# Two-level down-projection: weight loads moved to another queue, a block of sums moved, one large read cut in sixteen

## The chip, the cores and the metric

One core of a Trainium2 chip (trn2). The metric is the device time of one execution in microseconds. The kernel before takes 2875.6 us (median of three runs, 2875.38 to 2876.66).

## The reference, cut to what matters

The program is two whole blocks in fp32: an attention block with an MLP, then a pooling/recurrence block with a mixture of experts. The change touches the MLP of the first block and nothing else:

```python
h = rms_norm(x, norm_mlp) * (1 + sc_f) + sh_f          # 1024 tokens x 1024
x = x + g_f * (square(relu(h @ w_mlp_in)) @ w_mlp_out)  # 1024 -> 4096 -> 1024
```

## The kernel before, in words

Everything about the change is in `stage_out_mlp`. The products are Strassen-like: a 2x2 block product is made of seven products m1 to m7 of sums of blocks, so the tensor engine (PE) does fewer products and the vector engine (DVE) more additions. After the attention's output projection come two stages.

**The up stage** (h @ w_mlp_in, relu, square). There are 32 pairs: 2 halves of the tokens times 16 pairs of hidden columns (`FPAIRS`). A pair n is seven products in the order m1, m5, m6, m7, m2, m4, m3 (`up_pair`, `product`, line 1343), four fp32 matmuls each (a matmul of fp32 is two records in the trace, so a product is 8 records). For each pair:

- SyncE (SP) loads the pair's 1 MB of weights into one of two buffers `w1s[n % 2]` (`pair_weights`, line 1201). The load of pair n+1 takes the buffer of pair n-1, so it waits until PE has done pair n-1.
- DVE makes four sums of the weights (`sums_of`, lines 1538 to 1543). m5, m6, m7 and m3 read them; m1, m2 and m4 read the raw weights.
- DVE takes the products out of the eight PSUM banks (`gather`, `add`, line 1568): u2 (product m6), u3 (m7), u4 and c22 (m5, the third and fourth taking), c11 (m2), c21 (m4), c12 (m3). A product can only start when the product eight places earlier has been taken.
- ScalarE (ACT) copies m1, then clamps and squares the four corners c22, c11, c21, c12 (lines 1503, 1513, 1516). In pairs 1 to 4 it also takes turned activations of the second token half first (`take_h`). In the second half of the tokens SP stores the squares to `hid_rows` (`hidden_store`, line 1218).

In the DVE program of before, the sums of pair n+1 stand ahead of all takings of pair n (line 1786).

Beside this runs **the preparation of the down weights**, in 16 sub blocks s. SP loads a sub block of 1 MB (`sub_load`, lines 1208 and 1209: 768 and 256 KB), DVE makes 45 more blocks of it in four steps (`sub_sums`, lines 1580 to 1595), SP stores 3.1 MB to `t_rows` in DRAM (`sub_store`, line 1213), and the next `sub_load` waits until that store has landed, since there is one buffer. DVE has the steps at fixed places of its program: `between(i)` of pair n is place 7n+i, and sub block s has its four steps at `made_from(s) = 18 + 49*s//4` and the three places after it, that is one sub block every 12.25 products or 1.75 pairs. i runs 0 (ahead of u2), 1 (ahead of u3), 2, 3, 4 (ahead of c11), 5, 6 (ahead of c12), and the first steps of four sub blocks in a row fall on i = 4, 2, 0, 5. `sub_store` stands at place +5 of the SP program and the next `sub_load` at place +8; `hidden_store(n-1)` stands at place i = 3 of pair n. SP runs its program strictly in order, and all of its transfers are in one queue. After the last store SP reads the residual back (line 1260, 4 MB).

**The down stage** (@ w_mlp_out) runs 14 passes: 2 halves of the tokens times the 7 outer products `OUTER`, each pass of 8 quads of 7 products of one matmul (line 1385). SP loads 896 KB of `t_rows` for each quad into a ring of four buffers (`down_sums_in`, line 1231), each as soon as the quad four earlier is done. The first and the last two quads of a pass are interleaved product by product, so those are done nearly together. The activations of the second half come back from `hid_rows` by `hidden_load` (line 1236), two DMAs of 4 MB, issued in the SP program behind the loads of quads 43 and 51 (passes 5 and 6); pass 7 is the first that reads them. In the last pass PE also turns the first half of the residual, 8 blocks of 4 transposes (`turn_residual`, line 1399), into bank 7; ACT copies each out (line 1521) before the next.

Of the kernel before, what the change touches and what calls it, by code (L numbers as in the profile page):

```python
# [1031 lines left out]
def stage_out_mlp(nc, main, tail, early, w1, w2, w_head, t_rows, hid_rows, x_rows, xres, ada_acc, b_ada, cols, modc, gates, ones, ident):  # L1032
# [9 lines left out]
    with Scope(nc, "mlp") as s:  # L1042
# [136 lines left out]
        def operand_there(eng, g):  # L1179
            h, name = g // HALF_PASSES, OUTER[g % HALF_PASSES]  # L1180
            if name in ("m5", "m6", "m7", "m3"):
                eng.wait_ge(side_made, side_at(h, name))
            elif h:
                eng.wait_ge(hid_in[0 if name == "m1" else 1], 16)
            else:
                eng.wait_ge(squared, 4 * FPAIRS)

        ended_at = [0]
        for g in range(PASSES):
# [2 lines left out]
        with nc.Block() as block:  # L1192
            @block.sync
            def _(sp):
                def pair_weights(n):
                    if n == 1:
                        sp.wait_ge(out_part, len(out_parts))
                    if n >= 2:
                        sp.wait_ge(up, 7 * (n - 1))
                        sp.wait_ge(summed, 4 * (n - 1))  # L1200
                    sp.dma_start(w1s[:, n % 2, :, :], w1[n % FPAIRS]).then_inc(w1_in[n % 2], 16)

                def sub_load(s):
                    if s:
                        sp.wait_ge(sub_out, 16 * s)
                    else:
                        sp.wait_ge(parked, 16 * TT)
                    sp.dma_start(sub_all[:, 0:3, 0:4, :], w2[s // 2, s % 2, :, 0:3]).then_inc(sub_in, 16)
                    sp.dma_start(sub_12, w2[s // 2, s % 2, :, 3]).then_inc(sub_in, 16)

                def sub_store(s):
                    sp.wait_ge(sub_made, 8 * s + 8)
                    sp.dma_start(t_rows[:, s // 2, :, s % 2, :].rearrange("o p n -> p o n"),
                                 sub_all[:, :, 1:8, :].rearrange("p o i n -> p o (i n)")).then_inc(sub_out, 16)

                def hidden_store(n):
                    sp.wait_ge(squared, 4 * n + 4)
                    sp.dma_start(hid_rows[n - FPAIRS], staged[:, n % 2, :]).then_inc(hid_out[n % 2], 16)

                def down_sums_in(n):  # L1220
                    g, j = n // QUADS, n % QUADS
                    if n < RING:
                        sp.wait_ge(sub_out, 16 * SUBS)
                        sp.wait_ge(up, 7 * (2 * FPAIRS - 1 if n < 2 else 2 * FPAIRS))
                        sp.wait_ge(summed, 4 * (2 * FPAIRS - 1 if n < 2 else 2 * FPAIRS))
                    if n == 3:
                        for out in hid_out:
                            sp.wait_ge(out, 8 * FPAIRS)
                    if n >= RING:
                        quad_done(sp, (n - RING) // QUADS, (n - RING) % QUADS)  # L1230
                    sp.dma_start(ring[n % RING][:, 0:14 * P], t_rows[IN_PLACE[OUTER[g % HALF_PASSES]], j].rearrange("p c n -> p (c n)")
                                 ).then_inc(t_in[n % RING], 16)

                def hidden_load(o):
                    sp.wait_ge(side_made, side_at(0, "m7" if o == 0 else "m3"))
                    sp.dma_start(main[:, :, 2 * o * NB:(2 * o + 2) * NB],
                                 hid_rows.rearrange("(j o) p c -> o p j c", o=2)[o]).then_inc(hid_in[o], 16)

                for g, off in enumerate((2 * D, 5 * D)):
                    sp.dma_start(brow[:, g, :], b_ada[off:off + D].partition_broadcast(P)).then_inc(brow_in, 16)  # L1240
                pair_weights(0)
                pair_weights(1)
                sp.wait_ge(xn_done, TT)
                for t in range(TT):
                    sp.dma_start(x_rows[t * P:(t + 1) * P, :], xres[:, t, :]).then_inc(parked, 16)
                for n in range(2 * FPAIRS):
                    if 1 <= n < 2 * FPAIRS - 1:
                        pair_weights(n + 1)
                    for i in range(7):
                        at = 7 * n + i  # L1250
                        if at in sub_stores:
                            sub_store(sub_stores[at])
                        if at in sub_loads:
                            sub_load(sub_loads[at])
                        if i == 3 and n > FPAIRS:
                            hidden_store(n - 1)
                        if at == made_from(SUBS - 1) + 6:
                            sp.wait_ge(sub_out, 16 * SUBS)
                            for t in range(TT):
                                sp.dma_start(xres[:, t, :], x_rows[t * P:(t + 1) * P, :]).then_inc(x_back, 16)  # L1260
                    if n == 2 * FPAIRS - 1:
                        down_sums_in(0)
                        down_sums_in(1)
                hidden_store(2 * FPAIRS - 1)
                down_sums_in(2)
                down_sums_in(3)
                for n in range(RING, PASSES * QUADS):
                    down_sums_in(n)
                    if n == 5 * QUADS + RING - 1:
                        hidden_load(0)  # L1270
                    if n == 6 * QUADS + RING - 1:
                        hidden_load(1)
                    if n == 13 * QUADS + RING - 1:
                        sp.wait_ge(side_made, side_at(1, "m3"))
                        flat = w_head.rearrange("p n k c -> p (n k c)")
                        sp.dma_start(main[:, 2:6, HEAD_AT:2 * D], flat[:, 0:28 * P].rearrange("p (r c) -> p r c", r=4)).then_inc(head_in, 16)
                        sp.dma_start(main[:, 6, HEAD_AT:HEAD_AT + 4 * P], flat[:, 28 * P:32 * P]).then_inc(head_in, 16)
                sp.wait_ge(head_in, 32)

            @block.tensor  # L1280
            def _(pe):
# [120 lines left out]
                def down_pass(g):  # L1402
                    operand_there(pe, g)
                    last_pair = 2 * FPAIRS - 1
                    for i, name in enumerate(PRODUCTS):
                        if g:
                            pe.wait_ge(copied, 7 * (g - 1) + i + 1)
                        elif i == 0:
                            pe.wait_ge(part, part_at(last_pair - 1, "c12"))
                        elif i == 1:  # L1410
                            pe.wait_ge(taken, last_pair + 1)
                        else:
                            pe.wait_ge(part, part_at(last_pair, LAST_READ[PRODUCTS[i - 1]]))
                        for j in range(2):
                            down_product(g, j, name)
                    for j in range(2, QUADS - 2):
                        for name in PRODUCTS:
                            down_product(g, j, name)
                        if g == PASSES - 1:
                            turn_residual(2 * j - 4)  # L1420
                            turn_residual(2 * j - 3)
                    for name in PRODUCTS:
                        for j in range(QUADS - 2, QUADS):
                            down_product(g, j, name)
# [23 lines left out]
            def _(act):  # L1448
# [48 lines left out]
                for half in range(2):  # L1497
                    for j in range(FPAIRS):
                        n = half * FPAIRS + j
                        act.wait_ge(up, up_at(n, "m1"))  # L1500
                        if n:
                            act.wait_ge(part, part_at(n - 1, "c11"))
# [27 lines left out]
            def _(dve):  # L1530
# [66 lines left out]
                def gather(n, j, next_tokens):  # L1597
# [20 lines left out]
                    dve.wait_ge(part, part_at(n, "u3"))  # L1618
                    corner_free("c22")
                    add(n, "c22", corner["c22"], "m5", u3)  # L1620
                    between(4)
                    corner_free("c11")
                    add(n, "c11", corner["c11"], "m2", first_copy)
# [26 lines left out]
                def side_sums(g):  # L1650
                    h, name = g // HALF_PASSES, OUTER[g % HALF_PASSES]
                    X, Y = by_side
                    if name == "m5":
                        if h:
                            dve.wait_ge(hid_in[0], 16)
                            dve.wait_ge(hid_in[1], 16)
                            dve.wait_ge(whole, 7 * (g - HALF_PASSES + 3))
                        else:
                            dve.wait_ge(up, 14 * FPAIRS)
# [122 lines left out]
                for half in range(2):  # L1782
                    for j in range(FPAIRS):
                        n = half * FPAIRS + j
                        if n + 1 < 2 * FPAIRS:
                            every(sums_of(n + 1))
                        else:
                            inner_sums(0, 0)
                        gather(n, j, next_tokens if n == FPAIRS - 1 else iter(()))
                for g in range(PASSES):  # L1790
# [2011 lines left out]
```

## Time and profile before

| | before |
|---|---|
| median of three runs | 2875.6 us |
| the profiled execution | 2869.83 us, of which the span 2868.1 us |
| granted TensorE clock, whole span | 0.964 |
| PE busy | 2613.7 us, 91% |
| DVE busy | 1636.3 us, 57% |
| ACT busy | 871.7 us, 30% |
| DMA over the span | 476.06 MB, mean 166 GB/s |

The trace has the start of each instruction from the start of the span, its duration, and what an engine waited for before it. The granted clock is a share of 2.4 GHz. SPq is the issue of a DMA on SyncE; it is not the transfer. "8 records" of line 1343 are one product.

### The profile page before, as it was taken

To read this page: it belongs to the slowest core of one execution; us is meant where nothing else is said; L and a number is where in the kernel's file an instruction comes from. 1 tells how busy PE (TensorE), PEld (TensorE's weight loads), DVE (VectorE), ACT (ScalarE), POOL (GpSimd) and SP (SyncE) were. 2 spreads that over 40 slices of the span, in tenths; PEclk is the share of its full clock that TensorE was granted. 3 is DMA by queue.
4 is the path that set the end of the run, shared out by engine and by line. 5 is a ranking of instruction groups with operands and counts; after the bars stand their busy time and mean duration, and the time that the engine had idled before them with its cause. 6 is when DMAs were issued, how large, how long until landed. Compare 5 with 4: busy or idle time off the path is not lost. (4 is left out here: it accounts for less than half of the span.)

```text
span 2868.1 us, 55655 instructions
## 1 busy us (share of the span) xinstructions
PE 2613.7 (91%) x22330; PEld 1890.7 (66%) x22330; DVE 1636.3 (57%) x4094; ACT 871.7 (30%) x2171; POOL 305.5 (11%) x411
## 2 busy tenths in 40 slices
PE   6999999999887887779889998999999989999996
PEld 4888766654676666668778846777777755544443
DVE  5443277775544644544635536888888857522225
ACT  3111166642221221211011124666666610200002
POOL 0000023310000000000000000111111100353312
PEclk9999999999999988889999999999999989999998
DMA  5010143320355456578888731000000020599995
GB/s 237 31 59 30 59 159 122 126 97 1 124 209 229 185 221 239 210 265 308 327 305 300 304 151 61 28 28 28 3 28 28 18 107 30 206 394 402 401 383 198
DMA packets 138035, 476.06 MB, mean 166 GB/s; under 512 B 10928, under 2 KB 20656, under 8 KB 128832
## 3 DMA queue, kind: packets, MB, share of 16 engines
q1 hardware_dynamic: 129536, 447.99, 41.8%
q0 software_dynamic: 8256, 24.65, 2.3%
q8 instruction: 174, 2.85, 0.4%
q14 instruction: 69, 0.57, 0.1%
HBM read 375.55 MB, written 97.06 MB: 165 GB/s over the span
## 5 line engine op out<-in xcount | busy, mean ns | idle before, releaser
L2204 PE MATMUL mixing_ps<-all_main,pre_ws 64*64 64x256 f32 x3072 | 247.1, 379 | 0.0
L3291 PE MATMUL ex_ps<-all_main,ex_xT 128*128 128x512 f32 x496 | 223.4, 593 | 2.4 <-DVE ex_xT L3449 2.1
L1343 PE MATMUL mlp_ps<-all_main,all_early 128*128 128x256 f32 x512 | 141.4, 425 | 90.0 <-DMA all_early<-in_w 73.7
L1343 PEld LDWEIGHTS mlp_ps<-all_main,all_early 128*128 128x128 f32 x512 | 107.4, 213 | 112.7 <-DMA all_early<-in_w 79.3
L1513 ACT ACTIVATE all_gates<-all_gates 128x256 f32<-128x256 f32 x128 | 52.2, 408 | 381.0 <-DVE all_gates L1568 380.9
L1538 DVE TENSOR_TENSOR mlp_w2s<-all_early 128x512 f32<-128x512 f32 x32 | 22.0, 688 | 250.4 <-DMA all_early<-in_w 250.4
L3291 PEld LDWEIGHTS ex_ps<-all_main,ex_xT 128*128 128x128 f32 x496 | 91.7, 190 | 107.1 <-issue 100.7
L1343 PE MATMUL mlp_ps<-all_tail,mlp_w2s 128*128 128x256 f32 x512 | 131.2, 411 | 27.4 <-DVE all_gates L1568 27.4
L2204 PEld LDWEIGHTS mixing_ps<-all_main,pre_ws 64*64 64x64 f32 x3072 | 133.3, 134 | 19.3 <-issue 0.3
L1343 PEld LDWEIGHTS mlp_ps<-all_tail,mlp_w2s 128*128 128x128 f32 x512 | 106.9, 211 | 48.3 <-issue 29.1
L254 PE MATMUL qkv_ps<-qkv_wq,h_hT 128*128 128x256 f32 x576 | 134.3, 386 | 2.9 <-DVE h_hT L547 2.9
L1385 PE MATMUL mlp_ps<-mlp_w2s 128*128 128x256 f32 x448 | 126.2, 385 | 0.0
L254 PEld LDWEIGHTS qkv_ps<-qkv_wq,h_hT 128*128 128x128 f32 x576 | 111.5, 194 | 19.6 <-issue 4.1
L1343 PE MATMUL mlp_ps<-all_main,mlp_w2s 128*128 128x256 f32 x512 | 122.3, 382 | 0.0
L1385 PE MATMUL mlp_ps<-mlp_w2s,all_main 128*128 128x256 f32 x336 | 97.3, 385 | 19.3 <-DMA mlp_w2s<-t_rows 19.1
L3241 POOL DMA_INDIRECT all_main<-h_rows,ex_idx x112 | 106.6, 951 | 49.5 <-issue 27.0
L1890 POOL MEMSET pool_blank<- 128x1024 f32 x1 | 1.0, 954 | 1032.3 <-POOLq L60 1032.3
L1643 DVE TENSOR_TENSOR mlp_w2s<-all_main 128x512 f32<-128x512 f32 x28 | 19.4, 691 | 156.2 <-PE mlp_ps L1385 155.8
L1343 PEld LDWEIGHTS mlp_ps<-all_main,mlp_w2s 128*128 128x128 f32 x512 | 98.8, 193 | 13.9
L2626 DVE STREAM_TRANSPOSE all_tail<-all_tail 64x128 f32<-64x128 f32 (+1 forms) x336 | 100.5, 304 | 9.3
L2899 PE MATMUL mixing_ps<-all_main 128*128 128x512 f32 x224 | 102.2, 600 | 0.7 <-PEq L2136 0.7
L2468 ACT COPY all_tail<-mixing_ps 128x256 f32<-128x256 f32 (+2 forms) x264 | 86.2, 347 | 37.3 <-PE mixing_ps L2306 33.6
(512 smaller groups left out, 5680.0 us busy)
## 6 DMA issues: line engine op xcount, KB each, us to landing
all_main<-in_w_gu SPq DMA_DIRECT2D x31, 2048.0 KB, 14.9
t_rows<-all_xres SPq DMA_DIRECT2D x16, 3136.0 KB, 10.1
mlp_w2s<-t_rows SPq DMA_DIRECT2D x56, 896.0 KB, 6.1
all_early<-in_w SPq DMA_DIRECT2D x32, 1024.0 KB, 8.1
all_early<-t_rows SPq DMA_DIRECT2D x28, 896.0 KB, 6.2
all_tail<-t_rows SPq DMA_DIRECT2D x28, 896.0 KB, 5.5
att_wa<-in_w_ada SPq DMA_DIRECT2D x32, 512.0 KB, 3.9
all_early<-in_w_d SPq DMA_DIRECT2D x16, 1024.0 KB, 17.2
```

The lines of the kernel that those rows point to most:

```text
L254: last = nc.tensor.matmul(ps[:, bank_of[c, i, name], 0:HN], lhsT=weights(k), rhs=moving(k), start=k == 0, stop=k == HK - 1)
L1343: last = nc.tensor.matmul(ps[:, bank(n, name), 0:QB], lhsT=weights(k), rhs=moving(k), start=k == 0, stop=k == HK - 1)
L1385: last = nc.tensor.matmul(ps[:, PRODUCTS.index(name), 0:QB].rearrange("p (c t) -> p c t", c=2), lhsT=lhsT, rhs=rhs, start=j == 0, stop=j = ...
L1513: nc.scalar.activation(corner[name], corner[name], ACT.Relu).then_inc(clamped, 1)
L1538: yield nc.vector.tensor_tensor(S[0], A21, A22, ALU.add).then_inc(summed, 1)
L1643: nc.vector.tensor_tensor(s1, x21, x22, ALU.add).then_inc(in_made, 1)
L2204: last = nc.tensor.matmul(ps[heads(m), banks[half], 0:UT], lhsT=ws[heads(half), n, k, heads(m)], rhs=columns(k, heads(half)), start=(k == ...
L2468: nc.scalar.copy(dst, src).then_inc(steps.sem, 1)
L2626: ins_of(*args, **kw).then_inc(dve_w.sem, 1)
L2899: last = nc.tensor.matmul(ps[:, 2 * (t % 2) + n, :], lhsT=mixT[:, k, t * P:(t + 1) * P], rhs=ws[:, k, n * NB:(n + 1) * NB], start=(k == 0) ...
L3241: nc.gpsimd.indirect_dma_start(out=xg[:, n, a * QD:(a + 1) * QD], out_offset=None, in_=h_quarters, in_offset=bass.IndirectOffsetOnAxis(ap= ...
L3291: last = nc.tensor.matmul(pg[:, n % 2, :], lhsT=(xT[:, n % 2, :] if x is None else x)[:, k * P:(k + 1) * P], rhs=gu[n][:, k, :], start=(k ...
```

## The change

Four edits, all in `stage_out_mlp`. The up weights of pair n+1 are loaded from ScalarE's queue, at the start of its work for pair n, that is behind the squares of pair n-1; the first two loads stay on SP. DVE makes the sums of pair n+1 behind the fourth taking (c22) of pair n, no longer ahead of the first. The second half's activations are read in 16 DMAs of 512 KB, one behind the load of each of the quads 46 to 61. In the last pass the two turnings of a quad stand behind m5 and behind m2, no longer both behind m3.

```diff
--- before.py
+++ after.py
@@ -1181,9 +1181,17 @@
             if name in ("m5", "m6", "m7", "m3"):
                 eng.wait_ge(side_made, side_at(h, name))
             elif h:
-                eng.wait_ge(hid_in[0 if name == "m1" else 1], 16)
+                eng.wait_ge(hid_in[0 if name == "m1" else 1], 16 * QUADS)
             else:
                 eng.wait_ge(squared, 4 * FPAIRS)
+
+        def pair_weights(eng, n):
+            if n == 1:
+                eng.wait_ge(out_part, len(out_parts))
+            if n >= 2:
+                eng.wait_ge(up, 7 * (n - 1))
+                eng.wait_ge(summed, 4 * (n - 1))
+            eng.dma_start(w1s[:, n % 2, :, :], w1[n % FPAIRS]).then_inc(w1_in[n % 2], 16)
 
         ended_at = [0]
         for g in range(PASSES):
@@ -1192,14 +1200,6 @@
         with nc.Block() as block:
             @block.sync
             def _(sp):
-                def pair_weights(n):
-                    if n == 1:
-                        sp.wait_ge(out_part, len(out_parts))
-                    if n >= 2:
-                        sp.wait_ge(up, 7 * (n - 1))
-                        sp.wait_ge(summed, 4 * (n - 1))
-                    sp.dma_start(w1s[:, n % 2, :, :], w1[n % FPAIRS]).then_inc(w1_in[n % 2], 16)
-
                 def sub_load(s):
                     if s:
                         sp.wait_ge(sub_out, 16 * s)
@@ -1231,21 +1231,18 @@
                     sp.dma_start(ring[n % RING][:, 0:14 * P], t_rows[IN_PLACE[OUTER[g % HALF_PASSES]], j].rearrange("p c n -> p (c n)")
                                  ).then_inc(t_in[n % RING], 16)
 
-                def hidden_load(o):
+                def hidden_load(o, j):
                     sp.wait_ge(side_made, side_at(0, "m7" if o == 0 else "m3"))
-                    sp.dma_start(main[:, :, 2 * o * NB:(2 * o + 2) * NB],
-                                 hid_rows.rearrange("(j o) p c -> o p j c", o=2)[o]).then_inc(hid_in[o], 16)
+                    sp.dma_start(main[:, j, 2 * o * NB:(2 * o + 2) * NB], hid_rows[2 * j + o]).then_inc(hid_in[o], 16)
 
                 for g, off in enumerate((2 * D, 5 * D)):
                     sp.dma_start(brow[:, g, :], b_ada[off:off + D].partition_broadcast(P)).then_inc(brow_in, 16)
-                pair_weights(0)
-                pair_weights(1)
+                pair_weights(sp, 0)
+                pair_weights(sp, 1)
                 sp.wait_ge(xn_done, TT)
                 for t in range(TT):
                     sp.dma_start(x_rows[t * P:(t + 1) * P, :], xres[:, t, :]).then_inc(parked, 16)
                 for n in range(2 * FPAIRS):
-                    if 1 <= n < 2 * FPAIRS - 1:
-                        pair_weights(n + 1)
                     for i in range(7):
                         at = 7 * n + i
                         if at in sub_stores:
@@ -1266,10 +1263,10 @@
                 down_sums_in(3)
                 for n in range(RING, PASSES * QUADS):
                     down_sums_in(n)
-                    if n == 5 * QUADS + RING - 1:
-                        hidden_load(0)
-                    if n == 6 * QUADS + RING - 1:
-                        hidden_load(1)
+                    if 5 * QUADS + 6 <= n < 6 * QUADS + 6:
+                        hidden_load(0, n - 5 * QUADS - 6)
+                    if 6 * QUADS + 6 <= n < 7 * QUADS + 6:
+                        hidden_load(1, n - 6 * QUADS - 6)
                     if n == 13 * QUADS + RING - 1:
                         sp.wait_ge(side_made, side_at(1, "m3"))
                         flat = w_head.rearrange("p n k c -> p (n k c)")
@@ -1416,9 +1413,8 @@
                     for j in range(2, QUADS - 2):
                         for name in PRODUCTS:
                             down_product(g, j, name)
-                        if g == PASSES - 1:
-                            turn_residual(2 * j - 4)
-                            turn_residual(2 * j - 3)
+                            if g == PASSES - 1 and name in ("m5", "m2"):
+                                turn_residual(2 * j - 4 + ("m5", "m2").index(name))
                     for name in PRODUCTS:
                         for j in range(QUADS - 2, QUADS):
                             down_product(g, j, name)
@@ -1497,6 +1493,8 @@
                 for half in range(2):
                     for j in range(FPAIRS):
                         n = half * FPAIRS + j
+                        if 1 <= n < 2 * FPAIRS - 1:
+                            pair_weights(act, n + 1)
                         act.wait_ge(up, up_at(n, "m1"))
                         if n:
                             act.wait_ge(part, part_at(n - 1, "c11"))
@@ -1618,6 +1616,8 @@
                     dve.wait_ge(part, part_at(n, "u3"))
                     corner_free("c22")
                     add(n, "c22", corner["c22"], "m5", u3)
+                    if n + 1 < 2 * FPAIRS:
+                        every(sums_of(n + 1))
                     between(4)
                     corner_free("c11")
                     add(n, "c11", corner["c11"], "m2", first_copy)
@@ -1652,8 +1652,8 @@
                     X, Y = by_side
                     if name == "m5":
                         if h:
-                            dve.wait_ge(hid_in[0], 16)
-                            dve.wait_ge(hid_in[1], 16)
+                            dve.wait_ge(hid_in[0], 16 * QUADS)
+                            dve.wait_ge(hid_in[1], 16 * QUADS)
                             dve.wait_ge(whole, 7 * (g - HALF_PASSES + 3))
                         else:
                             dve.wait_ge(up, 14 * FPAIRS)
@@ -1782,9 +1782,7 @@
                 for half in range(2):
                     for j in range(FPAIRS):
                         n = half * FPAIRS + j
-                        if n + 1 < 2 * FPAIRS:
-                            every(sums_of(n + 1))
-                        else:
+                        if n + 1 == 2 * FPAIRS:
                             inner_sums(0, 0)
                         gather(n, j, next_tokens if n == FPAIRS - 1 else iter(()))
                 for g in range(PASSES):
```

## Rows read from the trace of the kernel before

**Rows 1.** Windows, the up stage: us, busy per engine (instructions), clock, DMA share, GB/s

```profile
737.00:1284.00 547.00, 429.59 (x1825) 365.47 (x1824) 275.42 (x495) 119.96 (x307) 0.00 (x0) 0.90 0.58 218
```

**Rows 2.** Waits, up stage, PE: us in total, times, longest

```profile
PE mlp_ps L1343 <- DMA all_early<-in_w: 73.7, 14, 16.1
PE mlp_ps L1343 <- DVE all_gates L1568: 43.7, 12, 8.8
```

**Rows 3.** Waits of SP's own queue, up stage

```profile
SPq L1213 <- DVE all_xres L1595: 266.4, 16, 21.0
SPq L1208 <- DMA t_rows<-all_xres: 142.0, 15, 10.7
```

**Rows 4.** Timeline around one PE stall: start us, us, engine, line, operation, records [idle before]

```profile
1120.60 0.38 SPq L1213 DMA_DIRECT2D t_rows<-all_xres  x1
...
1130.03 0.38 SPq L1208 DMA_DIRECT2D all_xres<-in_w  x1
...
1131.07 0.35 SPq L1201 DMA_DIRECT2D all_early<-in_w  x1
...
1139.37 0.69 DVE L1538 TENSOR_TENSOR mlp_w2s<-all_early 128x512 f32<-128x512 f32 x1 [16.81 <-DMA all_early<-in_w]
1139.39 1.22 PE L1343 MATMUL mlp_ps<-all_main,all_early 128*128 128x256 f32 x2 [8.29 <-DMA all_early<-in_w]
```

**Rows 5.** Timeline: two products, one clamping, steps of two sub blocks

```profile
1085.35 0.68 DVE L1580 TENSOR_TENSOR all_xres<-all_xres 128x512 f32<-128x512 f32 x1
...
1092.00 1.09 DVE L1595 TENSOR_TENSOR all_xres<-all_xres 128x896 f32<-128x896 f32 x1
...
1110.24 0.68 DVE L1580 TENSOR_TENSOR all_xres<-all_xres 128x512 f32<-128x512 f32 x1
...
1113.67 1.89 PE L1343 MATMUL mlp_ps<-all_main,all_early 128*128 128x256 f32 x8
...
1115.39 1.89 PE L1343 MATMUL mlp_ps<-all_tail,all_early 128*128 128x256 f32 x8
...
1121.66 0.42 ACT L1513 ACTIVATE all_gates<-all_gates 128x256 f32<-128x256 f32 x1 [6.98 <-DVE all_gates L1568]
```

**Rows 6.** Timeline, first and last of the 16 stores of sub blocks

```profile
796.30 0.38 SPq L1213 DMA_DIRECT2D t_rows<-all_xres  x1
...
1242.43 0.38 SPq L1213 DMA_DIRECT2D t_rows<-all_xres  x1
```

**Rows 7.** DMA issues: count, KB each, median us to landing; last, line 1201 alone

```profile
t_rows<-all_xres SPq DMA_DIRECT2D x16, 3136.0 KB, 10.1
...
all_xres<-in_w SPq DMA_DIRECT2D x16, 768.0 KB, 4.6
...
DMA to landing us min/median/max: 4.8/8.1/13.7
```

**Rows 8.** Timeline, a stall ahead of the first sub block, one behind the last

```profile
771.10 3.75 PE L1343 MATMUL mlp_ps<-all_main,all_early 128*128 128x256 f32 x8 [8.80 <-DVE all_gates L1568]
...
1269.05 0.69 DVE L1538 TENSOR_TENSOR mlp_w2s<-all_early 128x512 f32<-128x512 f32 x1 [24.66 <-DMA all_early<-in_w]
```

**Rows 9.** Timeline, down stage: ring loads that mark the ends of passes

```profile
1358.55 1.49 SPq L1231 DMA_DIRECT2D mlp_w2s<-t_rows  x1
...
1382.72 5.93 SPq L1231 DMA_DIRECT2D mlp_w2s<-t_rows  x2
...
1408.73 0.36 SPq L1231 DMA_DIRECT2D mlp_w2s<-t_rows  x1
...
1476.68 0.36 SPq L1231 DMA_DIRECT2D mlp_w2s<-t_rows  x1
```

**Rows 10.** Windows, down stage: without and with a read of 4 MB

```profile
1364.00:1384.00 20.00, 20.00 (x94) 17.64 (x93) 10.37 (x12) 2.60 (x7) 0.00 (x0) 1.00 0.80 299
...
1444.00:1464.00 20.00, 12.12 (x54) 10.31 (x53) 11.20 (x18) 0.00 (x0) 0.00 (x0) 0.88 1.01 409
```

**Rows 11.** Timeline, last pass: one of four second turnings

```profile
1634.80 0.65 PE L1399 MATMUL mlp_ps<-all_ident,all_xres 128*128 128x128 f32 x4 [0.68 <-ACT all_main L1521]
```

## The prediction

> **What bounds the kernel now.** I read the windows by stage first. The up stage takes 547 us at a granted clock of 0.90 [rows 1]. Then the pace of an undisturbed product: two neighbours start 1.72 us apart [rows 5], so seven are 12.1 us and the 224 products of 32 pairs 387 us; with 7 us for the turnings in it (eight at 0.9 us), PE needs 394 us. The stage thus loses 153 us. PE's waits name 117 of them: 73.7 for the weights themselves, 43.7 for DVE's takings [rows 2], and the rest is mostly the slow level behind a stall (8 records in 3.75 us at 1.2 GHz [rows 8], 1.89 at 2.4 GHz [rows 5]). The takings are late for the same reason: DVE stands ahead of all takings of a pair and waits for the next pair's weights. Then SP's own waits: 266.4 us for the last step of a sub block and 142.0 us for the landing of its store [rows 3]. One stall shows how these meet: the store leaves at 1120.60, SP stands at the next `sub_load` until 1130.03, and only then, at 1131.07, sends the weights whose buffer had been free since PE passed to the next pair, some 12 us before; DVE gets them at 1139.37 after 16.81 us, PE has stood for 8.29 us [rows 4]. So the bound of the stage is the order of SP's program. In the down stage an undisturbed pass is 24.17 us (1358.55 to 1382.72), and the two passes with the 4 MB reads take 67.95 us together (1408.73 to 1476.68), 19.6 more than two plain ones [rows 9].
>
> **Loads on ScalarE's queue: what comes next.** At the start of its pair n ACT has squared c12 of pair n-1, so PE and the sums are long past what the two added waits ask; they cost nothing, and behind them stand only the copy of m1 and the squares. The issue costs on SP 0.35 us [rows 4]; no row shows one on ACT. 30 of them lie in an engine busy for 120 of 547 us [rows 1], price 0 (bounds: below nothing is excluded, an issue cannot shorten ACT's work; above, 30 x 1.1 us, SP's longest issue, in the idle time anyway). Two loops are then left, and the longer one sets the stage.
>
> *Weight loop.* Load lands, four sums at about 0.61 us spacing, each 0.69 [rows 4]: 2.5 us; then c11, c21, c12, and ACT's three pairs of clamp and square at 0.8 us (twice 0.4 [rows 5]) behind c11: 2.9 us; then the next load. Steps of a sub block on places 4 to 6 come between: a sub block's steps are 7.1 us of DVE (4 x 0.68 + 4 x 1.08 [rows 5]), 4.0 us a pair, 3/7 of them there, of which ACT's lag hides a quarter: 1.3 us. The load: 4.8 us at best, 8.1 median, 13.7 worst, with SP's stores ahead of it in one queue [rows 7]. In a queue of its own it no longer stands behind 3.1 MB. 1 MB at the 409 GB/s that a full window moves [rows 10] is 2.6 us; alone 4.8, at half the rate 7.4; I take 7.0. Loop: 7.0 + 2.5 + 2.9 + 1.3 = 13.7 us a pair. PE wants 12.1.
>
> *Sub block loop.* Steps, store, load, one after the other in one buffer. The steps with the takings between them take 7.8 us from the first step to the store (1085.35 to 1093.1) or 10.4 (1110.24 to the store at 1120.60) [rows 4, 5]; half each, 9.1. The change keeps that: the sums leave one place and come into another (i = 2 now has them inside). The store takes 10.1 us to land [rows 7]; a weight load runs beside it now, 2.6 us of the same 16 DMA engines, in about three stores of four: 12.1. The next load takes 0.4 + 4.9, with the same sharing in four of ten cases 6.2. Sum 27.4 us for 1.75 pairs, 15.7 us a pair. It is the longer loop, and it is the next bound; DVE will stand at the first step of a sub block (L1580) for its load, which it never does now. Now a sub block takes (1242.43 - 796.30)/15 = 29.74 us [rows 6]. Fifteen intervals: 15 x (29.74 - 27.4) = **-35.1 us**.
>
> The Trainium skill, *DMA: Bandwidth & Descriptors*, "Queues, rings and completion order", says each DMA engine alternates between the queues that have work, packet by packet. That fits the half rate taken; no run here has shown two busy queues of this kind.
>
> **Sums behind the fourth taking.** Costs no DVE time. It frees u2, u3, u4 and c22 from the wait for weights, so PE's banks of m6, m7 and m5 come free on time; what then waits behind the weights is c11, c21 and c12, whose banks are needed only eight products (13.8 us) later, and through them the next load: that is in the weight loop above. With the loads in time it also delays S for m5 of the next pair: weights landing at 9 us of a 12.1 us pair give the first sum at 9.7, needed at 13.8. Price inside the loops 0; if the weights land late, m5 stands 1 to 5 us, once in two pairs, in the time that the sub block loop leaves PE idle anyway.
>
> **Both ends of the stage.** Ahead of the first sub block PE stands 8.8 us and pays 1.9 us at the slow level [rows 8], since the load of pair 2 is sent behind eight stores of x_rows. From ACT it is sent about 5 us earlier and lands beside them: that stall goes. By the durations above: the load of pair 2 is sent at 752.8 and lands at 760.5; that of pair 3 goes behind pair 1's squares, which ACT makes behind the two turned blocks, at 766.8, and lands at 773.8; sums to 776.3, the steps and takings 8.4 us, first store at 784.7 for 796.30: **-11.6**. Behind the last store, now at 1242.43, the stage takes 41.5 us more to 1283.9; in them the last weights stand behind the 4 MB residual, and DVE waits 24.66 us [rows 8]. With those weights sent by ACT, PE has 2.3 pairs left: 2.3 x 12.1 = 28 and a microsecond: 29. **-12.5**. Up stage: -59 us, 488 for 547.
>
> **Sixteen pieces.** Each quad of 3.02 us loads 0.9 MB, at a DMA share of 0.80: 2.4 us; a window full of the reads moves 409 GB/s at share 1.01 [rows 10], so 8.4 MB take 20.5 us, 1.28 us a piece. Over 16 quads the DMAs need 16 x (2.4 + 1.28) = 58.9 us and PE 48.3. 10.6 stay, less one to two us that the ring holds in store: 9. The two large reads now cost 19.6 [rows 9]. 19.6 - 9 = **-10.6** (bounds 0, the same bytes cost the same, and -19.6, all hidden). The pieces are all sent by quad 1 of pass 7, so pass 8 does not wait for them.
>
> **Turnings apart.** PE stands 0.68 us at the second turning of a quad, four times [rows 11]; with three products (1.3 us) between, ACT's copy is done: **-2.7**.
>
> **Sum.** -59.2 - 10.6 - 2.7 = -72.5; I give 2 us back for m1 and m5 run at the slow level where they are now on a path: -70.5. From the profiled execution (span 2868.1, 1.7 around it, 2869.8) that is 2799.3; the median of before is 5.8 us higher, and I state the forecast against it: 2875.6 - 70.5 = **2805**.
>
> **Rivals.**
> 1. *The sub block loop is shorter than I price it*, the two queues share without loss: 9.1 + 10.1 + 5.3 = 24.5. Then the weight loop (13.7 x 1.75 = 24.0) is as long, and 15 x (29.74 - 24.7) = 75.6 in place of 35.1: 2805 - 40.5 = 2764. For it: the DMA share of the stage is only 0.58 [rows 1]. Against: the loads must fall somewhere, and the store fills 12 of each 27 us. Chance 0.19.
> 2. *Moving the issue gives nothing, the transfers being what is late.* The weights land as late as now since the store and they need the same engines; only the down stage gains: 2875.6 - 13.3 = 2862. Against: of the 16.81 us in rows 4, 10 are SP's wait, in which the load was not sent. Chance 0.12. The Trainium skill, same page, "Issuing engines are not separate DMA queues", says issuing from several engines only saves the sequencer's time; by that rule this is the result. The 142.0 us of rows 3 are just time of the sequencer, so row and rule can both hold.
> 3. *Slower: the weight loop closes on itself.* Before, a load waited for PE alone; now it waits for squares that wait for c12, that waits for the sums, that wait for the load before. If the store holds the load back as it does in one queue (4.26 MB at 409 GB/s and the 2.2 us of a load alone that are not bytes: 12.6; worst seen 13.7 [rows 7]), the loop is 12.6 + 6.7 = 19.3 us a pair, 618 us in place of 547: +71, less 13.3 in the down stage: 2933. It decides from a landing of 10.4 us on, where the loop is today's 17.1 a pair; with the gains of the down stage from 10.8. For it: nothing here shows how two queues share. Chance 0.07.
> 4. *Same:* the landing at that point, 0.02.
>
> **How the numbers follow.** Forecast 0.60, own range 2784 to 2830 (a loop of 26 to 29, pieces -5 to -17). The range takes in half of rival 1 and stops short of rivals 2 and 3: 2760 to 2852. About 0.2% is what a measurement here can tell. Faster 0.91, same 0.02, slower 0.07.
>
> **What the profile after would show.** SP's wait for a landed store stays, but no weights stand behind it; L1201 issues on ACT. The longest wait of DVE is for the sub block's load at L1580 and for weights at L1538 of some 3 to 5 us a time, not 14 to 25. Stores of sub blocks 27 us apart; the stage near 488 us; PE's clock still under 1. Passes 5 and 6 near 58 us together; no idle at the second turning. If the stores come 25 us apart, rival 1; if L1201 takes over 10 us to land with the stage over 547, rival 3; if L1538 waits as before, rival 2.

## The result

The changed kernel takes 2796.2 us (median of four, 2793.1 to 2797.7) for 2875.6: ratio 0.9722, 95% interval 0.9705 to 0.9739, 79 us less. The forecast was 2805 (range 2760 to 2852). The time came out as foreseen; two of the reasons given for it did not hold, and the experiments below took them apart.

Of the page of the changed kernel, the time by engine and two of its DMA issues:

```profile
span 2791.3 us, 55669 instructions
...
PE 2605.0 (93%) x22330; PEld 1878.7 (67%) x22330; DVE 1637.7 (59%) x4094; ACT 876.9 (31%) x2171; POOL 305.9 (11%) x411
...
t_rows<-all_xres SPq DMA_DIRECT2D x16, 3136.0 KB, 11.3
...
all_early<-in_w ACTq DMA_DIRECT2D x30, 1024.0 KB, 7.2
```

The work is the same and the span is 76.8 us shorter. The up stage in windows (same columns as [rows 1]), and PE's and DVE's waits in it, answering [rows 2]:

```profile
736.50:1209.20 472.70, 416.92 (x1825) 355.61 (x1823) 279.02 (x497) 125.87 (x309) 0.00 (x0) 0.94 0.68 252
```

```profile
PE mlp_ps L1340 <- DMA all_early<-in_w: 37.5, 16, 5.8
PE mlp_ps L1340 <- issue: 14.2, 6, 6.1
PE mlp_ps L1340 <- DVE all_gates L1566: 2.5, 1, 2.5
```

```profile
DVE mlp_w2s L1536 <- DMA all_early<-in_w: 84.0, 19, 7.5
DVE all_xres L1578 <- DMA all_xres<-in_w: 44.3, 12, 9.0
```

The stage is 472.7 us for 547, at a granted clock of 0.94 for 0.90. PE's waits for takings fell from 43.7 to 2.5 us, those for weights from 73.7 to 37.5 (14.2 more are at m5, for the first of the sums, and stand under "issue"). DVE now waits at L1578 for a sub block's load, which it never did. The first and the last store of a sub block, answering [rows 6]:

```profile
782.46 0.38 SPq L1213 DMA_DIRECT2D t_rows<-all_xres  x1
...
1178.43 0.38 SPq L1213 DMA_DIRECT2D t_rows<-all_xres  x1
```

They are (1178.43 - 782.46)/15 = 26.40 us apart for 29.74, and PE begins the down stage 30.8 us behind the last for 41.7. SP still waits for the landing of the stores, as in [rows 3], and longer:

```profile
SPq L1213 <- DVE all_xres L1593: 215.9, 16, 16.7
SPq L1208 <- DMA t_rows<-all_xres: 163.3, 15, 13.4
```

One turn of the weight loop, from the timeline (ACTq is the issue of a DMA on ScalarE):

```profile
841.91 0.33 ACTq L1194 DMA_DIRECT2D all_early<-in_w  x1
...
850.51 0.69 DVE L1536 TENSOR_TENSOR mlp_w2s<-all_early 128x512 f32<-128x512 f32 x1 [6.21 <-DMA all_early<-in_w]
850.53 1.99 PE L1340 MATMUL mlp_ps<-all_main,all_early 128*128 128x256 f32 x8 [2.24 <-DMA all_early<-in_w]
...
853.05 0.42 DVE L1566 TENSOR_TENSOR all_gates<-mlp_ps,mlp_spare 128x256 f32<-128x256 f32 x1
...
856.25 0.42 DVE L1566 TENSOR_TENSOR all_gates<-mlp_ps,mlp_small 128x256 f32<-128x256 f32 x1
...
857.14 0.42 ACT L1514 ACTIVATE all_main<-all_gates 128x256 f32<-128x256 f32 x1
857.21 0.33 ACTq L1194 DMA_DIRECT2D all_early<-in_w  x1
```

Load out at 841.91, landed at 850.5, four sums, c11 at 853.05, c12 at 856.25 with steps of a sub block between, its square, and the next load at 857.21: 15.3 us round, with PE standing 2.24.

### The profile page after: what moved, and what is told of

Its sections match the earlier page's. It is cut to its first block and busy times, and to the rows that moved or that the text cites. A ratio compares the mean times of both kernels' runs of the same rounds, so it can differ in the third digit from the quotient of the medians.

```text
span 2791.3 us, 55669 instructions
## 1 busy us (share of the span) xinstructions
PE 2605.0 (93%) x22330; PEld 1878.7 (67%) x22330; DVE 1637.7 (59%) x4094; ACT 876.9 (31%) x2171; POOL 305.9 (11%) x411
## 5 line engine op out<-in xcount | busy, mean ns | idle before, releaser
L1340 PE MATMUL mlp_ps<-all_main,all_early 128*128 128x256 f32 x512 | 132.8, 405 | 40.1 <-DMA all_early<-in_w 37.5
L1340 PEld LDWEIGHTS mlp_ps<-all_main,all_early 128*128 128x128 f32 x512 | 101.2, 201 | 61.9 <-DMA all_early<-in_w 44.2
L1340 PE MATMUL mlp_ps<-all_tail,mlp_w2s 128*128 128x256 f32 x512 | 126.5, 404 | 14.3 <-issue 14.2
L1382 PE MATMUL mlp_ps<-mlp_w2s,all_main 128*128 128x256 f32 x336 | 97.4, 384 | 12.4 <-DMA mlp_w2s<-t_rows 10.9
L1382 PEld LDWEIGHTS mlp_ps<-mlp_w2s 128*128 128x128 f32 x448 | 86.1, 193 | 12.0
## 6 DMA issues: line engine op xcount, KB each, us to landing
t_rows<-all_xres SPq DMA_DIRECT2D x16, 3136.0 KB, 11.3
```

The source lines that it names most:

```text
L1340: last = nc.tensor.matmul(ps[:, bank(n, name), 0:QB], lhsT=weights(k), rhs=moving(k), start=k == 0, stop=k == HK - 1)
L1382: last = nc.tensor.matmul(ps[:, PRODUCTS.index(name), 0:QB].rearrange("p (c t) -> p c t", c=2), lhsT=lhsT, rhs=rhs, start=j == 0, stop=j = ...
```

## Experiments

All were timed in three rounds against the kernel before. "Up stage" is from the first product of pair 0 to the first product of the down stage.

### Which of the two edits of the up stage did it

`e3_down_only`: only the edits of the down stage. Its diff against the changed kernel takes back both of these:

```diff
-                        if 1 <= n < 2 * FPAIRS - 1:
-                            pair_weights(act, n + 1)
...
+                    if 1 <= n < 2 * FPAIRS - 1:
+                        pair_weights(sp, n + 1)
...
-                    if n + 1 < 2 * FPAIRS:
-                        every(sums_of(n + 1))
...
+                        if n + 1 < 2 * FPAIRS:
+                            every(sums_of(n + 1))
```

> The kernel before with only the edits of the down stage: 16 pieces and turnings apart. Theory: passes 5 to 7 take 85.2 us as in the changed kernel for 93.0, the turnings give 2.7: 10.5 us less, 2865, and the 5 us by which other passes of the changed kernel were longer belong to that execution or to the up stage. Rival: the pieces or the earlier end cost those 5 us in the other passes too: 2870.

Measured: 2864.4 us, ratio 0.9968 (0.9950 to 0.9985), 9 us less. The theory (2865) was right. Its down stage takes 361.9 us for 371.8 before, and its up stage 549 for 547.

`e1_sums_back`: of the two, only the sums are put back; the loads stay on ScalarE's queue.

> The changed kernel with one part undone: the sums of pair n+1 stand again ahead of all takings of pair n; the loads stay on ScalarE's queue. Theory (the weight loop closes over DVE and ACT): land 7.0, sums 2.5, seven takings 2.7, steps of sub blocks 4.0, last squares 1.5 us make 17.7 us a pair, no better than the 17.1 of before: the up stage takes 530 to 566 us for 472.7 in the changed kernel, 2855 to 2885 us in all. Rival (the queue alone does the work): up stage within 10 us of the changed kernel's, 2796 to 2806 us.

Measured: 2898.0 us, ratio 1.0076 (1.0053 to 1.0100). **The change of queue alone makes the kernel slower**, by 34 us against `e3_down_only`; the up stage takes 577 us, more than the 530 to 566 that I had put it at. Its loads land in 8.5 us in the median, so the queue is not slow; they leave late. One turn in its timeline:

```profile
1011.14 0.69 DVE L1536 TENSOR_TENSOR mlp_w2s<-all_early 128x512 f32<-128x512 f32 x1 [5.49 <-DMA all_early<-in_w]
...
1016.96 3.41 PE L1340 MATMUL mlp_ps<-all_tail,mlp_w2s 128*128 128x256 f32 x8 [3.80 <-DVE all_tail L1549]
...
1022.66 0.42 ACT L1511 ACTIVATE all_gates<-all_gates 128x256 f32<-128x256 f32 x1 [15.66 <-DVE all_gates L1566]
...
1025.44 0.33 ACTq L1194 DMA_DIRECT2D all_early<-in_w  x1
...
1033.61 0.69 DVE L1536 TENSOR_TENSOR mlp_w2s<-all_early 128x512 f32<-128x512 f32 x1 [8.85 <-DMA all_early<-in_w]
```

From landed weights to the next load 14.3 us (this pair also has token sums in it): all takings of the pair and all four squares lie between. The load's 8 us come on top, 22.5 us in this turn; over the whole stage a pair takes 18.0 us (577 / 32) for the 17.7 of the theory.

`e2_loads_back`: of the two, only the loads are put back on SP.

> The changed kernel with the other part undone: loads of up weights on SyncE again at their old place, sums behind the fourth taking. Theory: PE's 43.7 us of waits for takings go, the 73.7 us of waits for weights stay, as SP still stands at the store of a sub block: up stage about 505 to 515 us, 2830 to 2842 in all. Rival (the place of the sums does the work, queue irrelevant): up stage under 480 us, 2796 to 2806 in all.

Measured: 2792.0 us, ratio 0.9709 (0.9679 to 0.9739), the same as the changed kernel. The rival was right: **the place of the sums alone brings the whole gain**, 72 us beyond `e3_down_only`. SP's order had not changed here, and yet PE's waits for weights fell. First PE's waits in `e3_down_only`, then PE's and DVE's in this run:

```profile
PE mlp_ps L1342 <- DMA all_early<-in_w: 73.2, 14, 16.9
PE mlp_ps L1342 <- DVE all_gates L1566: 39.1, 11, 8.7
```

```profile
PE mlp_ps L1342 <- DMA all_early<-in_w: 43.4, 11, 13.6
PE mlp_ps L1342 <- issue: 14.4, 5, 4.1
...
DVE mlp_w2s L1536 <- DMA all_early<-in_w: 66.4, 9, 17.6
```

The windows of both up stages (columns as in [rows 1]), `e3_down_only` first:

```profile
736.50:1285.50 549.00, 436.77 (x1825) 370.15 (x1825) 275.21 (x494) 120.01 (x307) 0.00 (x0) 0.88 0.57 217
```

```profile
740.00:1215.00 475.00, 416.99 (x1824) 358.50 (x1824) 276.82 (x494) 121.77 (x307) 0.00 (x0) 0.94 0.67 251
```

The stage is 74 us shorter: 39 us of waits for takings are gone, 30 of those for weights, 14 came at m5 (for the sums), and PE is busy for 20 us less with the same products, at a granted clock of 0.94 for 0.88.

The stores of its sub blocks are 25.5 us apart (790.95 to 1173.96), nearer than in the changed kernel. Counted from the first product of the stage, the changed kernel wins 5 us ahead of the first store and 10 behind the last, and gives 13 back in between, so its up stage is 3 us shorter; its down stage is 6 us longer (366.3 for 360.0).

### Was SyncE's order a bound at all

`e5_pool_loads` sends the loads of pairs 2 to 31 from GpSimd, which has nothing else to do in this stage, and `e8_pool_sums_back` does so with the sums at the old place:

```diff
+            @block.gpsimd
+            def _(pool):
+                for n in range(1, 2 * FPAIRS - 1):
+                    pair_weights(pool, n + 1)
```

> As the run with loads on GpSimd's queue, but the sums of the next pair ahead of all takings again, as in the kernel before. It tells apart what bound the kernel before. Theory A (SyncE's order, on which the prediction rested): with the loads out of SP's order and out of the squares' way most of the gain is there without moving the sums: up stage 485 to 500 us for 547, 2805 to 2825 in all. Theory B (DVE's order: it stands for the next weights with all takings behind it): up stage 530 us or more, 2845 to 2870.

Measured: 2805.0 us, ratio 0.9757 (0.9738 to 0.9776), up stage 486 us. Theory A gave this, at the lower end of its range. So a load that waits for neither SP's stores nor ScalarE's squares brings 59 us beyond `e3_down_only` with the sums unmoved; its loads land in 5.3 us in the median for 8.3, and DVE waits 56.5 us for them for 254.7 in `e3_down_only`. How much of the 59 us is the earlier issue and how much the shorter landing, no run separates. The loss of the kernel before had two links, SP late with the load and DVE standing for it with all takings behind it, and cutting either one takes most of it away. The cut must not close a new loop: with the loads on ScalarE's queue and the sums unmoved (`e1_sums_back`) it did.

> The changed kernel with the loads of up weights of pairs 2 to 31 on GpSimd's queue, which waits for nothing but PE and the sums, not for ScalarE's squares. Theory (in the changed kernel the loop over the squares holds the loads back): loads leave 2 to 6 us sooner, PE's 37.5 us of waits for weights in the up stage mostly go, 25 to 35 us less: 2761 to 2771. Rival (the sub block loop is the bound): stores of sub blocks stay 26.4 us apart, 2790 to 2800.

Measured: 2795.2 us, ratio 0.9724 (0.9708 to 0.9740), no gain over the changed kernel. The rival was right, and the waits say how: PE's for weights are gone, and the sub block's load takes their place.

```profile
PE mlp_ps L1345 <- issue: 57.6, 10, 10.9
...
PE mlp_ps L1345 <- DMA all_early<-in_w: 0.3, 1, 0.3
```

```profile
DVE all_xres L1586 <- DMA all_xres<-in_w: 107.7, 16, 13.3
```

The stores stay 26.6 us apart (782.51 to 1182.05). DVE stands at the sub block with the sums behind it, and PE stands at m5 for the sums; the longest wait in the timeline shows it, though the profile files it under "issue":

```profile
1012.29 0.69 DVE L1586 TENSOR_TENSOR all_xres<-all_xres 128x512 f32<-128x512 f32 x1 [13.30 <-DMA all_xres<-in_w]
...
1015.50 0.68 DVE L1544 TENSOR_TENSOR mlp_w2s<-all_early 128x512 f32<-128x512 f32 x1
...
1016.28 2.05 PE L1345 MATMUL mlp_ps<-all_tail,mlp_w2s 128*128 128x256 f32 x4 [10.92 <-issue]
```

The weight loop had been freed; the sub block loop held.

### Cutting the sub block loop, three times in vain

`e4_split_store` cuts each store of a sub block in two; the next load waits for the first part alone:

```diff
+                    for lo, hi, done in ((0, 3, sub_first), (3, 7, sub_out)):
+                        sp.dma_start(t_rows[lo:hi, s // 2, :, s % 2, :].rearrange("o p n -> p o n"),
+                                     sub_all[:, lo:hi, 1:8, :].rearrange("p o i n -> p o (i n)")).then_inc(done, 16)
```

> The changed kernel with each store of a sub block cut into two DMAs (3 and 4 of 7 outer blocks); the next sub block's load waits for the first alone. Theory (the sub block loop is the bound now): its store term falls from about 11 to 6.5 us, stores come 24 us apart for 26.4, then the weight loop of 13.7 us a pair sets them: 15 x 2.4 = 36 us less, 2760; DVE's waits for the sub block's load (44.3 us) go nearly to nothing. Rival (the weight loop is already the bound): no change, 2790 to 2800.

Measured: 2792.5 us, ratio 0.9716 (0.9685 to 0.9748): no gain. Its DMA issues:

```profile
t_rows<-all_xres SPq DMA_DIRECT2D x16, 1344.0 KB, 4.9
...
all_xres<-in_w SPq DMA_DIRECT2D x16, 256.0 KB, 10.9
```

SP waits only 66.0 us for landed stores, but the load then lands in 10.9 us for 5.8 in the changed kernel: it stands behind the second part in SP's queue. 4.9 + 10.9 = 15.8 us from the store's issue to the landed load, for 11.3 + 5.8 = 17.1 in the changed kernel. The stores stay 26.5 us apart, although the exchange is 1.3 us shorter: the weight loads now land in 8.3 us for 7.2, and PE waits 44.5 us for them for 37.5. The wait moved. So this run did not decide what it was made for.

`e6_sub_pool` and `e7_sub_pool_sp` send the sub block's load from GpSimd's queue, so that no bytes stand ahead of it in its own; the latter has the weights back on SP.

> The changed kernel with each sub block's store in two DMAs and the next sub block's load on GpSimd's queue behind the first of them, so that it stands behind no bytes of the second. From the store's issue to the landed load 16.7 us in the changed kernel (15.8 with the store cut alone); here about 5 + 6 = 11. Theory (sub block loop is the bound): stores 24 us apart for 26.4, 36 us less, 2760. Rival (it is not): 2790 to 2800.

> The same cut of the sub block loop, but the up weights' loads back on SyncE's queue, where now no wait for a landed store stands ahead of them. Theory: both loops are cut, stores 22.5 to 24 us apart, up stage about 440 to 450 us, 2755 to 2765. Rival (transfers share the engines, so something always lands late): 2785 to 2800.

Measured: 2798.0 us (ratio 0.9738, 0.9717 to 0.9759) and 2798.6 (0.9751, 0.9724 to 0.9778): no gain. The load in a queue of its own still lands late:

```profile
all_xres<-in_w POOLq DMA_DIRECT2D x16, 256.0 KB, 10.5
```

4.9 + 10.5 = 15.4 us; in `e7_sub_pool_sp` the load takes 11.1, together 16.0. The expected 11 us were wrong, and so were both theories: stores came 26.7 and 26.1 us apart. The first store part, the load and the second part still share the engines, with the weights besides. In neither run is it shown what each queue got; what is shown is that the buffer's exchange takes 15 to 17 us in any order of the same transfers, as long as all of it lies between two groups of steps.

### Opening both loops

`e9_early_act` changes what lies between. The blocks 1 to 3 of each group are ready after the second of the four steps and are stored then; the next load needs only them to have landed and DVE to be done, and the rest of the store goes behind that load. Only the third step of the next sub block waits for it.

```diff
+                        if at - 3 in sub_firsts:
+                            sub_store(sub_firsts[at - 3], 1, 4, 4, sub_first)
+                        if at in sub_stores:
+                            if sub_stores[at] + 1 < SUBS:
+                                sub_load(sub_stores[at] + 1)
+                            sub_store(sub_stores[at], 4, 8, 8, sub_out)
```

> The changed kernel with the sub block loop opened: the blocks that are ready after the second of four steps are stored at once, and the next sub block's load goes behind the fourth step, beside the store of the rest, for which only the next block's third step waits. Load weights as changed, from ScalarE. Theory (in the changed kernel the weight loop and the sub block loop are about equally long, so freeing one alone gave nothing): now the weight loop of 13.7 us a pair is left, up stage about 445 to 460 us for 472.7, 2765 to 2785. Rival (something common to all, bytes or DVE, is the floor): 2790 to 2800.

Measured: 2766.9 us, ratio 0.9617 (0.9590 to 0.9644), up stage 445 us, as the theory had it. PE waits 32.8 us, all for weights: the weight loop is what is left.

`e10_early_pool` has GpSimd's loads of weights besides:

> Both loops opened: sub blocks as in the run with the early store, and the up weights of pairs 2 to 31 from GpSimd's queue, which does not wait for squares. Theory (two loops, nothing else): sub block loop about 19 us for the 21.2 that PE needs, so PE sets most of it, up stage 410 to 435 us, 2735 to 2760. Rival (a floor common to all): 2785 to 2800.

Measured: **2716.6 us**, ratio 0.9436 (0.9409 to 0.9463), the fastest of all and better than the theory's 2735 to 2760. Its up stage in windows (columns as in [rows 1]), and PE's only wait in it:

```profile
736.50:1138.80 402.30, 396.54 (x1827) 347.07 (x1825) 278.64 (x497) 122.10 (x307) 16.10 (x30) 0.99 0.83 296
```

```profile
PE mlp_ps L1353 <- issue: 5.4, 2, 2.9
```

The window is 402 us, the stage itself 401 by its first products; PE is busy for 396.5 of it, at a clock of 0.99: PE is the bound of the stage now. Each loop freed alone gave 1 us (`e5_pool_loads`, no more than noise) and 29 us (`e9_early_act`); together 80.

`e11_early_sp` has the weights on SP:

> The early store with the up weights loaded from SyncE's queue as in the kernel before, sums behind the fourth taking. SyncE now waits for no long store, so its order costs little. Theory: as with GpSimd's queue within 10 us, 2740 to 2770. Rival (SyncE's order still holds the weights back): 2780 to 2800.

Measured: 2749.2 us, ratio 0.9557 (0.9527 to 0.9588), in the range of the theory, but 33 us from GpSimd's queue where it had said 10, so SP's order still costs something: PE waits 28.2 us for weights. It is 18 us better than ScalarE's queue.

`e12_open_sums_back` is `e10_early_pool` with the sums at the old place:

> The kernel with both loops opened (early store, loads on GpSimd's queue), but the sums of the next pair again ahead of all takings. What is the place of the sums worth when nothing else is late? Theory: the load leaves at the start of a pair and lands 7.7 us later, DVE stands for it until 8 us into the pair and then has takings, sums and steps to make up, so c22's bank comes free up to 3 us late in every second pair: 20 to 40 us more than with the sums behind the fourth taking, 2737 to 2757. Rival (the place only mattered since the loads were late): within 8 us of 2717.

Measured: 2763.9 us, ratio 0.9625 (0.9609 to 0.9641): 47 us more, above the theory's 20 to 40 and far from the rival. The place of the sums is worth something of its own, since PE then waits for banks:

```profile
PE mlp_ps L1353 <- DVE all_gates L1582: 27.8, 10, 5.7
```

## Why the prediction was right, and where it was not

- **What bounds the kernel.** I called the order of SP's program the bound. `e8_pool_sums_back` shows it was one of two links; `e2_loads_back` shows that most of the loss goes with SP's order untouched. Rows 2 to 4 show the chain in the order of one stall, and there SP's wait comes last; that SP itself was waiting for DVE (the 266.4 us of [rows 3]), which was waiting for weights, I read and did not follow round. A ring of waits has no first member, and can be cut at any link.
- **Sums behind the fourth taking: price 0.** This step failed. Alone it brings 72 us. I saw that it frees PE's banks (the 43.7 us of [rows 2]) and put that inside the loops. By bank waits alone it should have been some 44 us. The rest is 30 us less of waits for weights, of which 14 come back at m5, and 20 us that PE is busy less at the higher granted clock. That weights come sooner because the steps of the sub blocks, and with them SP's stores and loads, do so fits the stores (25.5 us apart for 29.9) but was not tested by itself.
- **Loads on ScalarE's queue: the source of the gain.** This step failed too. Alone it costs 34 us, and beside the moved sums it gives nothing that can be told (2796.2 and 2792.0). Rival 3 named the mechanism, loads gated by squares that wait for the load before, but I made it hang on a slow landing. Landings were fast (7.2 us median, 9.8 at most, where I took 7.0), and what decides it is how many takings lie between landed weights and the last square.
- **The two loops.** Right. I gave 27.4 us for the sub block loop; stores came 26.4 apart. Of its terms the store was 11.3 for 12.1. I gave 13.7 us a pair for the weight loop, 24.0 for 1.75 pairs; `e9_early_act`, where it is the only one left, takes 445 us for the stage, 13.9 a pair. By these lengths opening the weight loop alone should give nothing (`e5_pool_loads`: 1 us) and opening the sub block loop alone at most 15 x (26.4 - 24.0) = 36 us (`e9_early_act`: 29). What the sum lacked is that the two meet: when the exchange of the sub block got 1 to 2 us shorter in `e4_split_store` and `e6_sub_pool`, the weights landed 1 us later and the stores stayed as far apart.
- **Both ends of the stage.** Ahead of the first store -13.8 us for my -11.6, behind the last -10.9 for -12.5.
- **Up stage in sum.** -74.3 us (472.7 for 547.0) for my -59.2: nearly all of the difference is the one microsecond in each of 15 intervals.
- **Sixteen pieces.** -10.6 foreseen. In the changed kernel passes 5 to 7 take 85.2 us for 93.1, 7.9 less, but passes 0 to 3 take 5.7 more (104.1 for 98.4), so that its down stage is only 5.5 shorter (366.3 for 371.8). `e3_down_only` has 83.5 us in passes 5 to 7, 9.6 less. The term holds. The prediction had no term for the early passes: they take 98.4 to 100.4 us in the five kernels that load the up weights from SP and 99.7 to 104.2 in the nine that don't, one execution each, so the longer early passes seem to go with the moved queue and not with the pieces or the sums. By what way is open; the first two loads of the ring land 9.6 and 10.2 us after their issue in the changed kernel, 5.6 and 7.3 before.
- **Turnings apart.** -2.7: at the second turnings PE does not wait any more, seen in the timeline of the last pass, but the term was not measured by itself.
- **Rival 2** did not come true: 2796.2 us, not 2862. Its rule in the Trainium skill (*DMA: Bandwidth & Descriptors*, "Issuing engines are not separate DMA queues") says another issuing engine saves only the time that the sequencer takes to start the DMA. The runs do not agree: an issue takes 0.3 to 0.5 us here, and by the issuing engine alone `e8_pool_sums_back` gains 59 us and `e1_sums_back` loses 34. Those come with the waits that stand ahead of the issue in each engine's program and, in `e8_pool_sums_back`, with the shorter landing. Only beside the moved sums did the queue make no difference (`e2_loads_back`).

The number came out although the shares were wrong: I gave the gain of a ring of waits to the link that I had cut in thought first. A calculation that has both edits in it and prices the loops that remain does not need the shares. Some luck was in it too: the up stage gave 15 us more than foreseen and the down stage 8 less, and these errors partly cancel.

## What to carry to other kernels

When waits form a ring (load, sums, takings, store, load), don't price edits by the engine whose wait is longest: compute the round time of each ring that is left after the edit, and expect that two edits of one ring do not add up (72 us for the sums alone, 59 for the loads alone, 69 for both, the loads on GpSimd's queue) while two rings of nearly equal length give little until both are opened. A DMA's issue inherits every wait of the engine that issues it, so put it on an engine that waits for exactly what frees the buffer; here the idle GpSimd was worth 50 us over ScalarE once the sub block loop was open, and 1 us before. A store that frees a buffer should leave in parts, each as soon as it is made, with the next load ahead of the last part.

## What the runs showed of the hardware

- Two busy queues shared the engines without holding each other up for long: beside the stores of 3.1 MB the weight loads landed in 7.2 us in the median and 9.8 at most, and the stores in 11.3. With the same order of sums and all in one queue (`e2_loads_back`) it was 7.2, 13.9 at most, and 10.0: the second queue took away the worst landings, not the median, and cost the stores 1.3 us.
- An issue cost ScalarE 0.33 us in the median (0.334 to 0.396, 30 of them); the same loads cost SP 0.38 (0.33 to 1.13) in the kernel before and GpSimd 0.53 (0.53 to 0.77) in `e5_pool_loads`.
- Behind part of a store in one queue (`e4_split_store`) or in a queue beside it (`e6_sub_pool`), the load landed within 0.4 us of the same time (10.9 and 10.5).
